# Seven block products for the in-projections of two feed-forward stages, and three additions in place of one reduction in the opening modulation

## The reference, cut to what matters

```
h = h + 0.5 * rms_norm(swiglu(rms_norm(h, g1), w_ffn1_in, w_ffn1_out), g1_post)   # 528 columns
h = h + rms_norm(mixer(rms_norm(h, gm)), gm_post)
h = h + 0.5 * rms_norm(swiglu(rms_norm(h, g2), w_ffn2_in, w_ffn2_out), g2_post)   # 512 columns
swiglu(x, w_in, w_out):  a, b = split(x @ w_in);  return (silu(a) * b) @ w_out     # d_ff = 2816
mod = silu(c) @ w_mod + b_mod                                                      # opening of the first block
```

## Time and profile before

| what | value |
|---|---|
| median of 3 runs | 2245.35 us (2240.53 to 2245.5) |
| profiled execution: own time | 2243.71 us |
| profiled execution: span | 2241.9 us |
| PE busy, DVE busy | 94%, 44% of the span |
| ACT busy, POOL busy | 32%, 28% |
| mean granted clock of PE | 0.950 of full speed |

### The profile page before, as it was taken

How to read it: one execution, slowest core, us unless ns; L and a number is a source line. 1 busy time by engine, 2 the same in 40 slices (tenths; PEclk the granted TensorE clock), 3 DMA queues, 4 the chain that set the end, 5 groups by cost and what they waited for, 6 DMA issues and landing times.

```text
span 2241.9 us, 28339 instructions
## 1 busy us (share of the span) xinstructions
PE 2103.8 (94%) x11650; PEld 1754.6 (78%) x11650; DVE 993.0 (44%) x1483; ACT 725.9 (32%) x919; POOL 624.9 (28%) x152
## 2 busy tenths in 40 slices
PE   4999989999979999989999997999999979999997
PEld 3697777888757666589999996878788768888885
DVE  7374587656366666442222326232333252223224
ACT  6531345222245555332121123343232232221222
POOL 1331323344200000024433441221244314444440
PEclk6998999999979999989999997999999969999997
DMA  8122114554127999612222221211122212222220
GB/s 257 39 76 93 57 57 132 188 178 160 38 94 277 343 346 341 211 57 77 93 94 94 83 85 38 76 38 57 57 94 94 94 38 94 94 94 94 94 94 38
DMA packets 175177, 261.03 MB, mean 116 GB/s; under 512 B 12169, under 2 KB 140858, under 8 KB 175086
## 3 DMA queue, kind: packets, MB, share of 16 engines
q1 hardware_dynamic: 173550, 257.65, 34.5%
q10 hardware_dynamic: 1536, 2.10, 0.3%
HBM read 257.62 MB, written 2.11 MB: 116 GB/s over the span
## 4 chain that ended last, share of the span: by engine, by line
PE 89%; DVE 8%; ACT 2%; issue 1%; DMA 1%; DVEq 0%; SPq 0%; ACTq 0%
PE PS L704 68%; PE PS L1236 7%; PE PS L1258 4%; DVE Hf L2101 1%; PE PS L1390 1%; DVE macc L2167 1%; DVE Hf L2082 1%; PE PS L1202 1%; PE PS L764 1%; PE PS L1278 1%; DVE R L2113 1%; PE PS L1342 1%; PE PS L779 1%; PE PS L906 0%; PE PS L1160 0%
## 5 line engine op out<-in xcount | busy, mean ns | idle before, releaser
L663 POOL TENSOR_TENSOR w_lo<-w_raw,w_hi 128x2048 fp32r<-128x2048 f32 x133 | 620.3, 4664 | 1527.9 <-ACT w_hi L1509 1527.9
L704 PE MATMUL PS<-HH,w_hi 128*128 128x512 f32 (+1 forms) x1936 | 602.9, 349 | 31.8 <-DVE HL L2075 27.3
L704 PE MATMUL PS<-HL,w_hi 128*128 128x512 f32 (+1 forms) x1936 | 600.6, 348 | 0.0
L704 PE MATMUL PS<-HH,w_lo 128*128 128x512 f32 (+1 forms) x1936 | 597.6, 346 | 0.0
L1509 ACT ACTIVATE w_hi<-w_raw 128x2048 fp32r<-128x2048 f32 x133 | 254.8, 1915 | 713.5 <-DMA w_raw<-in_w_ffn_in 296.0
L704 PEld LDWEIGHTS PS<-HH,w_hi 128*128 128x128 f32 x1936 | 339.8, 191 | 84.4 <-issue 35.9
L704 PEld LDWEIGHTS PS<-HH,w_lo 128*128 128x128 f32 x1936 | 339.4, 191 | 45.8
L704 PEld LDWEIGHTS PS<-HL,w_hi 128*128 128x128 f32 x1936 | 339.3, 191 | 44.8
L2798 DVE TENSOR_TENSOR actf<-PS,sg 128x528 f32<-128x528 f32 (+1 forms) x44 | 30.8, 699 | 428.8 <-PE PS L704 428.8
L2809 DVE TENSOR_TENSOR yacc<-yacc,PS 128x528 f32<-128x528 f32 (+1 forms) x176 | 122.3, 695 | 106.2 <-PE PS L704 106.2
L2691 DVE TENSOR_TENSOR m_lo<-m_raw,m_hi 128x2048 fp32r<-128x2048 f32 x56 | 128.3, 2292 | 77.5 <-ACT m_hi L1842 76.8
(11 more groups left out here) (429 smaller groups left out, 2583.9 us busy)
## 6 DMA issues: line engine op xcount, KB each, us to landing
w_raw<-in_w_in SPq DMA_DIRECT2D x49, 1024.0 KB, 5.0
w_raw<-in_w_ffn_in SPq DMA_DIRECT2D x44, 1024.0 KB, 4.9
m_raw<-in_w_exp_gate SPq DMA_DIRECT2D x56, 512.0 KB, 4.2
m_raw<-in_w_exp_up SPq DMA_DIRECT2D x56, 512.0 KB, 5.3
m_raw<-in_w_exp_down SPq DMA_DIRECT2D x56, 512.0 KB, 4.8
w_raw<-in_w_ffn_out SPq DMA_DIRECT2D x22, 1024.0 KB, 4.8
mod_late<-in_w_mod SPq DMA_DIRECT2D x16, 1024.0 KB, 5.3
mod_early<-in_w_mod SPq DMA_DIRECT2D x8, 1024.0 KB, 11.8
```

Of the source, the lines that this page charges most:

```text
L663: pool.tensor_tensor(w_lo[:, s, :], w_raw[:, s, :], w_hi[:, s, :].bitcast(F32), ALU.subtract).then_inc(split, 1)
L704: ins = mm(o, l, r, **k)
```

## The change

**Weights and h in blocks.** In every gate and up chunk of both stages, the 256 x 1024 by 1024 x T product is cut into 2 x 2 blocks: outputs in two halves of 128, features in two halves of four tiles k, columns in two halves of H = T/2. Seven block products (`seven_products`) take the place of eight: 7 x 4 x 3 = 84 matmuls of H columns in a chunk. They go to four PSUM slots, two to a slot, the seventh alone. The down chunks stay as they were.

**Sums of weights.** DVE makes four sums per gate or up chunk (`weight_sums`), each of 512 values per partition with two inputs in SBUF: three blocks into a new tile `wx_raw`, one in place in `w_raw`. ACT's `next_hi` waits for the second of them, not for the transfer, and makes a second hi part `wx_hi` of 1536 values; POOL makes `wx_lo` of 1536 values behind `w_lo` (`split_seven`). PE needs `wx_hi` and `wx_lo` from product 3 on. DVE makes the sums of a gate chunk between the gate's and the up's results of a unit, and those of an up chunk behind the fourth tile of a down chunk; those of chunks 0 and 1 of a stage behind tiles 4 and 6 of the stage in front, those of chunk 2 at the head of the stage.

**Sums of h.** In place of the 8 + 8 tile copies of `HH` and `HL`, ACT makes 12 copies, DVE 4 lo parts and 3 sums and POOL 3 lo parts and 1 sum (`split_blocks`, both `h_blocks`), all of the sums and lo parts over 4H values. DVE's and POOL's have two inputs in SBUF each.

**Results.** ACT copies the first product from PSUM to `fp` (H values); DVE makes seven additions of H values (`block_sums`), each with one input in SBUF and one in PSUM, into `sg` for a gate and into `actf` for an up chunk. Silu then runs once over 2T values in SBUF. DVE multiplies `actf` by `sg` once over 2T values, ACT copies the product to `ah` (DVE did), and DVE subtracts once over 2T values for `al`. `actf` and `sg` move into the space of `Hf`.

**Opening.** `mod_sum` makes three additions in place, of 1024, 512 and 256 values, each waiting for the one before.

```
+            def weight_sums(c):
...
+                dve.wait_ge(w_in_sem[s], 16 * (c // RING + 1) + more * 16)
+                a11, a12, a21, a22 = weight_blocks(w_raw[:, s, :])
+                x = wx_raw[s]
+                tt(x[:, 1], a11, a21, ALU.subtract)
+                tt(a21, a21, a22, ALU.add).then_inc(wn_ready, 1)
+                dve.wait_ge(wn_ready, n + more * 2)
+                L(tt(x[:, 0], a21, a11, ALU.subtract))
+                tt(x[:, 2], a12, x[:, 0], ALU.subtract).then_inc(wx_ready, 1)
...
+            def split_seven(c, s, more=0):
+                pool.wait_ge(wx_ready, seven_made(c) + 1 + more * 2)
+                split_chunk(c, s, more)
+                pool.wait_ge(hix_done, seven_made(c) + 1 + more * 2)
+                pool.tensor_tensor(wx_lo[s][:, :, :, :], wx_raw[s][:, :, :, :], wx_hi[s][:, :, :, :].bitcast(F32),
+                                   ALU.subtract).then_inc(splitx, 1)
...
+            def h_blocks(n, T):                                     # POOL
+                pool.wait_ge(hh_ready, base + KT)
+                pool.tensor_tensor(HL[:, 4:8, 0:H], Hf[:, 4:8, 0:H], HH[:, 4:8, 0:H].bitcast(F32), ALU.subtract).then_inc(hp_ready, 1)
+                pool.tensor_tensor(HXr[:, 1, :, 0:H], Hf[:, 4:8, H:T], Hf[:, 0:4, H:T], ALU.subtract).then_inc(t3_ready, 1)
...
+                def ups(n, par, more=0):                            # DVE
+                    block_sums(actf)
+                    dve.wait_ge(gate_silu, base + n + 1)
+                    tt(actf[:, :, 0:T], actf[:, :, 0:T], sg[:, :, 0:T], ALU.mult).then_inc(actf_ready, 1)
+                    dve.wait_ge(ah_ready, base + n + 1)
+                    tt(al[:, par, :, 0:T], actf[:, :, 0:T], ah[:, par, :, 0:T].bitcast(F32), ALU.subtract).then_inc(moe_act, 1)
...
+                def unit(n, c, par):                                # DVE
+                    gates()
+                    if c is not None:
+                        weight_sums(c)
+                    ups(n, par)
+                    down(None if c is None else c + 1)
...
+            def seven_products(T, h_from=None):                     # PE
+                for n in range(7):
+                    if n == 3:
+                        pe.wait_ge(splitx, xcount["n"] + 1 + xcount["more"])
...
+                    for k in range(4):
+                        for x, (l, r) in enumerate(((0, 0), (0, 1), (1, 0))):
+                            ins = product(PS[:, s, n % 2, 0:H], left[l][n][:, k, :], right[r][n][:, k, :],
+                                          start=k == 0 and x == 0, stop=k == 3 and x == 2)
...
             def mod_sum(n):
-                v_.tensor_reduce(macc[:, d % 2, :].unsqueeze(2), mod_early[n][:, :, :].rearrange("p k n -> p n k"), AX, ALU.add).then_inc(
-                    macc_ready, 1)
+                L(tt(raw[:, 0:4, :], raw[:, 0:4, :], raw[:, 4:8, :], ALU.add))
+                L(tt(raw[:, 0:2, :], raw[:, 0:2, :], raw[:, 2:4, :], ALU.add))
+                tt(macc[:, d % 2, :], raw[:, 0, :], raw[:, 1, :], ALU.add).then_inc(macc_ready, 1)
```

More of the change, by code:

```diff
@@ L1505, in next_hi @@
                 rounds = hi["rounds"]
-                act.wait_ge(w_in_sem[c % RING], 16 * (c // RING + 1) + rounds * 16)
+                if seven(c):
+                    act.wait_ge(wn_ready, seven_made(c) + 1 + rounds * 2)
+                else:
+                    act.wait_ge(w_in_sem[c % RING], 16 * (c // RING + 1) + rounds * 16)
                 if c >= RING:
@@ L1942, in swiglu @@
+                for n in range(2 * pairs + 1, units):
+                    unit(n, n % 2)
                     next_hi()
                     W.skip(KT)
-            norm(TALL, every)
+                next_hi()
+                W.skip(KT)
+                n_["ff"] += units
+            norm(TALL, every, split="blocks")
             swiglu(FF_UNITS, TALL)
@@ L2043, in _ @@
             norm(SEQ, y_real, split=False)
-            norm(SEQ, real, tiles=False)
-            swiglu(FF_UNITS, SEQ, last=True)
+            norm(SEQ, real, tiles=False, split="blocks")
+            swiglu(FF_UNITS, SEQ)
             norm(SEQ, y_real, split=False)
@@ L2806, in down @@
+                def down(then=None):
                     for m in range(KT):
@@ L2809, in down @@
                         W.release(tt(y, y, ps(s, T), ALU.add))
[L2811 to L2814, removed]
+                        if m == 3 and then is not None:
+                            weight_sums(then)
+                dve.wait_ge(hp_ready, 3 * f + 3)
+                gates()
+                weight_sums(at_ + 3)
+                ups(0, 0)
+                pairs = (units - 1) // 2 - 1
+                g0, l0, f0 = W.g, L.n, n_["fp"]
+                def unit(n, c, par):
+                    gates()
+                    if c is not None:
+                        weight_sums(c)
+                    ups(n, par)
+                    down(None if c is None else c + 1)
                 with dve.Fori(0, pairs) as i:
                     W.g, L.n = g0, l0
[L2817 to L2826, removed]
+                    W.more, L.more, n_["rounds"] = i * 8, i * 16, i * 2
+                    unit(i * 2 + 1, at_ + 5, 1)
+                    unit(i * 2 + 2, at_ + 8, 0)
+                assert L.n - l0 == 16, L.n - l0
+                W.g, L.n, n_["fp"] = g0 + 32 * pairs, l0 + 16 * pairs, f0 + 4 * pairs
+                W.more = L.more = n_["rounds"] = 0
+                for n in range(2 * pairs + 1, units):
+                    c = at_ + 3 * n + 2
+                    unit(n, c if n + 1 < units else None, n % 2)
+                down()
                 units_done["n"] += units
@@ L2839, in _ @@
             real = lambda k: R[:, k, META:TALL]
-            norm(TALL, every, c2(0))
-            swiglu(FF_UNITS, TALL)
+            norm(TALL, every, c2(0), split="blocks")
+            swiglu(0, FF_UNITS, TALL)
             norm(TALL, lambda k: yacc[:, k, 0:TALL], lambda k: gain1[:, k:k + 1], post=every)
```

266 lines of the change are left out of this document (205 added, 61 removed).

## The result

The changed kernel takes **2337.1 us** (median of 4 runs, 2329.5 to 2339.4) against 2245.4 before (2240.5 to 2245.9): ratio **1.041**, 95% interval 1.038 to 1.0435. It is slower by 92 us, where I had forecast 63. That is 1.1 us beyond the upper end of the range. The profiled execution's own time is 2339.4 (span 2337.4), 95.7 over the one of before; its granted clock is 0.926 of full speed (0.950).

The account below looks back on a forecast made before the run. PE was taken to bound the kernel, at 89% of the span. Terms -59.0, -2.2, +61, +16.8, +6.0, +1.2, +24, +7 and +8 summed to +62.8 on 2243.7, forecasting 2306 us, range 2256 to 2336.

Parts of the forecast that it names:

- PE, -59.0: Gate and up chunks of both stages: 84 matmuls a chunk save 32.2 us in A and 26.8 in B.
- Opening, -2.2: Start of the kernel: three additions replace each reduction; the last small addition waits for POOL, leaving 2.2 us saved.
- the bound of -6.5: Opening's other bound: the sixth sum ends at 41.2 us, without its last addition waiting for POOL.
- Steady waits, +61: Units 1 to 9: POOL holds the multiplication and `al`, so PE waits 3.2 us a unit in A, 3.6 in B.
- The rivals that rest on DVE not being held, at 2194 and 2260: Steady units: DVE isn't held, 2194 us (12%); or one of two blocks remains, waits half as long, 2260 (8%).
- Entry of A, +17.4: Norm ahead of stage A ends 16.8 us later through held weight sums and late squares; wider first h part adds 0.6.
- Entry of B, +6.6: Norm ahead of stage B: additions of squares behind POOL's two subtractions, +6.0 us; wider first h part adds 0.6.
- First chunks, +24 and the clock's +7: Start of each stage: h's operations exclude one another and sums and memsets follow, +12 us a stage; half-clock stretches, +7.
- Clock, +8: Behind steady pauses: half of nine in B lose full clock at about 1.7 us each, none in A.
- the third rival, "the clock goes in every unit": Steady units: all eighteen pauses cost 1.7 us of clock, 31 instead of 8, giving 2330 us; chance 15%.

Follow-up runs that it names:

- number five: The changed kernel with `al` behind four additions to `yacc` and the second chunk's block sums behind the sixth addition: 2230.6 us, 0.995 of before.
- number four: The changed kernel with POOL's subtractions for the next gate chunk held until `al` is done and the second chunk's block sums behind the eighth tile: 2257.3 us.
- number two: The changed kernel with DVE's `al` subtraction moved behind the first four additions to `yacc`, nothing left out: 2247.9 us, 1.002 of before.
- number three: The changed kernel with DVE's `al` subtraction moved behind only the first of the eight additions to `yacc`: 2288.4 us, 1.021 of before.

## Why the prediction was right, and where not

- **PE, -59.0**: right. -60.7 by the units of number five, where nothing else stands in the way.
- **Opening, -2.2**: the size was off, -3.7 at the first product. The smallest addition asked at 40.74 and got in before POOL, which shows from 40.90. The lock took 3.07 us from the next operation with two SBUF inputs instead, and the bound of -6.5 was missed for the same reason as forecast.
- **Steady waits, +61**: right in mechanism and nearly in size. Number four shows the lock, number two the chain behind it. Measured 30.4 in A (28.8 predicted) and 36.2 in B (32.4). The landing and ACT's copy came as the sum had them, within 0.5 us. The rivals that rest on DVE not being held, at 2194 and 2260, find nothing in these rows.
- **Entry of A, +17.4 with the wider h part**: +17.9. The squares were to end at 978.5 by before's clock and the additions near 983.4; less the opening's 3.4 that is 980.0, and they ended at 980.48.
- **Entry of B, +6.6**: +6.0. The additions of squares asked at 1854.03 and took 6.43 us behind POOL's two subtractions.
- **First chunks, +24 and the clock's +7**: about right. Number five leaves 14.3 us in A and 15.4 in B for the two together, where 15.5 each were forecast. In the changed kernel PE's pauses there are 9.6 us in A and 8.8 in B, and the clock was at half behind the third one in both.
- **Clock, +8**: the step that failed. I took "half of nine in B" and "none in A", from a pause of 2.92 that kept the clock and one of 3.87 that lost it, with 1.7 us a loss. In the trace eight of nine were lost in A, behind pauses of 3.25 to 3.51, and all nine in B. A loss is worth 1.4 to 1.5 us in A (35.80 against 37.3 inside the changed kernel, 34.5 against 35.9 in number three), once 2.7 (38.5, the first unit), and 2.3 in B. That makes 7 x 1.5 + 2.7 + 9 x 2.3 = **34 us** for 8. Added to the sum it gives 2332. With 5.4 us of longer pauses it is 2338, the measured time to within 2 us.

A check by another way: units 1 to 9 take 46.2 us (A) and 59.8 us (B) longer in the changed kernel than in number five, where PE's clock is full. The pauses are 30.4 and 36.2 of that, so 39.4 us are left, 5.5 more than the losses' price. A rest of that kind stands in number three's units at full clock too: 34.05 us less a pause of 2.5 is 31.5 in B, against 30.93 in number five. So part of it at least comes with a pause and not with the clock; its cause stays open.

So the third rival, "the clock goes in every unit", priced at 31 us and 2330, was all but the case (17 of 18), and I had given it 15%. Two things were wrong in how I weighed it. Two pauses at two places don't place a limit between them; the runs show that there is no sharp one (below). And the price of a loss came from one pause on other work, 1.7 us, where B's units lose 2.3. And the range ended at 2336, 6 us above this rival's time, so that little else could run over.

What the experiments add to the explanation: the seven products do bring their 60 us, and the loss of 92 is a matter of place. In the kernel before, the multiplication read one operand from PSUM (L2798, 0.70 us a tile) and was never held. It stood ahead of the additions to `yacc` there too, and so did `al`, which was held once in 44 times (1340.10). The change made the multiplication read two operands from SBUF, and in units 1 to 9 both operations now come while POOL is at work. `al` isn't needed so early: in number two it runs behind four of the additions, and PE's pauses over 3 us are gone.

## What to carry to other kernels

Where one engine's operation can be held by another's, look first at what stands behind it in its own list. An operation that nobody needs soon belongs behind those that free a buffer. Moving the one who holds (number four) took back 80 us here, but the lock then held the next operations in the list. Price a stall of PE together with the clock that it may cost behind it: here 3.4 us of waiting mostly cost 4.9 in A, and 4 us cost over 6 in B.

## What the runs showed of the hardware

- **The clock behind a pause has no sharp limit.** Kept at 1.00: behind 3.42 us once, and behind 14 of 18 pauses of 1.8 to 2.7. Lowered: behind eight pauses of 3.25 to 3.51, and behind four of those 18, two of them 2.00 and 1.93 us long. Pauses of like length in like units differ from one to the next. The fall doesn't come at one place either: it came 1.0 us ahead of the end of B's pause at 2031.39, and 1.3 us behind the end of A's at 1356.66.
- **How long the half clock lasts varies.** In the changed kernel the granted clock was still 0.50 five us behind a pause of B (window 2031.5 to 2036.5) and back at 1.00 by 2037.3. In A it rose within 3.9 us of the ends of the pauses at 1132.67, 1170.06 and 1207.33, but was 0.50 until past 1064 behind the one that ends at 1058.28.
- **One input in SBUF can be enough to be held.** A product of 128x8 values with a constant (one input in SBUF) took 4.49 us beside POOL's subtraction and 0.16 alone; eight memsets ran beside one at 0.55 us each. The Trainium skill says under "SBUF — State Buffer", section "SBUF: two separate sides", that operations in a two-port mode take the lock as well as those with two SBUF inputs. The held product fits that; which mode it ran in, no run here shows.
- **The lock passes in the order of asking**, in all 36 meetings of the multiplication and `al` in units 1 to 9: each waits for the one subtraction that runs, never for two. POOL gets its turn in the same way: at A's entry its `wx_lo`, ready at 963.28, went ahead of DVE's next sum, which came at 963.79 and ended at 967.69.
- **The same code differs by 5.6 us between executions** over the 360 us of the mixer, with the granted clock at 0.98 or 1.00: the slower one has 10 us at 0.50 from 1502.5 on, the faster none.
